# Forget-gate logits with the gate weights stationary in four column tiles of the array, summed and turned back by two products with a picking matrix

## The chip, the cores and the metric

One core of one Trainium2 chip. The time is the device time of one execution in microseconds; lower is better. TensorE (PE) multiplies, VectorE (DVE), ScalarE (ACT) and GpSimd (POOL) do the rest, SyncE (SP) issues most of the DMA transfers.

## What is computed

The reference is a model of two layers on 256 tokens of width 1024, all in float32. Each layer is a modulated norm, an attention block, a second norm and a mixture of 32 experts, of which each token uses two. The change touches one small piece of layer 0: eight of its sixteen attention heads have forget gates. Their logits are the last eight columns of the input projection, and their running sum over the tokens goes into the scores.

```python
proj = h @ w_in                       # h: 256 x 1024; w_in: 1024 x 3080, the last 8 columns are fb
log_f = jax.nn.log_sigmoid((fb + b_f).astype(jnp.float32))
cum_f = jnp.transpose(jnp.cumsum(log_f, axis=1), (0, 2, 1))
...
s = (jnp.einsum('bqhd,bkhd->bhqk', qb[:, i0:i1], kb[:, :i1]).astype(jnp.float32) * scale
     + (cum_f[:, :, i0:i1, None] - cum_f[:, :, None, :i1]))
```

## The kernel before

The program is written engine by engine, with semaphores between them; nothing reorders it. The activations of a layer lie turned in `m.hT`: 128 partitions by 8 chunks of the model width by 256 tokens. Dense weights come in units of 2 MB through a ring of six slots, in the order of `DENSE_ORDER`; SyncE issues a unit's transfer when the slot is free (`ring_used`).

In layer 0, once `m.hT` is ready, TensorE runs `project_early`: six items, each one unit's 512 columns for one half of the tokens (8 products of 128x512, line 642). Unit in0 gives items 0 and 1, in1 items 2 and 3, in2 items 4 and 5. Between them stand:

- after item 0, `forget_gates` (line 650): for each half of the tokens 8 products with a 128x128 piece of `m.hT` stationary and the 128x8 gate weights moving, so that the 128x8 logits lie with tokens on partitions;
- after items 1 and 3, `mod_products` of the group GATE1 (line 607): 8 products with 32 columns of the conditioning vector stationary, in four column tiles of 32 columns, moving 512 columns of weights;
- from item 2 on, `turn_qk` (line 697): transposes of queries and keys that VectorE has normed;
- after item 4, `forget_sums` (lines 658 to 664): the running sums, as products with a triangular matrix. Then attention starts (`scores`, line 734), with the other six items spread over its steps.

A product in float32 shows as two instructions in the trace. ScalarE copies each item out (`copy_item`), does the exponential and the logarithm of the gates (`f_abs`, `f_exp`) right after item 0, and the square root of each norm (`root8`). VectorE waits for the logits (`forget`, line 1407), then norms items 0 to 3 (`norm_qk`, lines 1426 to 1451). It has one order too: `forget` stands ahead of `norm_qk(0)`.

The small inputs, the gate weights among them, are loaded by ScalarE's queue at the start (`small_loads`, line 543); `forget_gates` waits for all nine of them on TensorE, and VectorE waits for them before it makes the rotary angles. After attention comes the router (line 844), and then the experts of the layer, whose weights stream through eight slots of 2 MB.

Of the kernel before, what the change touches and what calls it, by code (L numbers as in the profile page):

```python
# [26 lines left out]
P = 128  # L27
# [132 lines left out]
class Chain:  # L160
# [5 lines left out]
    def link(self, ins):  # L166

        self.n += 1
        ins.then_inc(self.sem, 1)
        self.eng.wait_ge(self.sem, self.n + self.more)  # L170
# [6 lines left out]
def allocate(nc, ctx):  # L177
    m = Machine()

    def sb(name, shape, dt=F32):  # L180
        return ctx.enter_context(nc.sbuf_tensor(name, shape, dt))

    def sem(name):
# [36 lines left out]
    m.cos, m.sin = (m.region[:, 6 * D + COL + 64 * i:6 * D + COL + 64 * (i + 1)].rearrange("p (t e) -> p t e", t=TT)  # L220
                    for i in range(2))
    m.head_g = m.region[:, 6 * D + COL + 128:6 * D + COL + 384].rearrange("p (i e) -> p i e", i=4)
    m.f_w = m.region[:, 6 * D + COL + 384:6 * D + COL + 448].rearrange("p (k h) -> p k h", k=KC)

    m.raw = [m.work[:, i * COL:(i + 1) * COL] for i in range(2)]
# [33 lines left out]
    m.cum_q = sb("cum_q", [P, TT, 8])  # L260
    m.cum_k = m.h[:, 1, 0:T]
    m.log_f2 = m.h[:, 1, T:2 * T].rearrange("p (t h) -> p t h", t=TT)
    m.sq_sum = sb("sq_sum", [P, 8])
    m.rstd = sb("rstd", [P, 8])
    m.low = sb("low", [P, NHH, TT])
# [26 lines left out]
    m.dve_step = sem("dve_step")  # L292
    m.act_step = sem("act_step")
    m.pool_step = sem("pool_step")
    names = """consts eps_ready gate_b_clear rows_ready c_act_done c_ready part_ready cols_made cols_ready row_made row_ready
        rstd_done h0_ready h1_ready hT_turned hT_dve hT_act
        proj_done proj_copied var8_ready rstd8_done qk_normed qk_turned qk_copied f_out f_abs f_exp f_ln f_ready cum_done cum_copied
        ang_ready trig_done lam_ready lam_exp
# [162 lines left out]
def program_pool(pool, m):  # L461
# [5 lines left out]

    pool.memset(m.eps[:, :], EPS).then_inc(m.s["eps_ready"], 1)
    pool.memset(m.ones[:, :], 1.0).then_inc(done, 1)
    pool.memset(m.gate_b[:, :], 0.0).then_inc(m.s["gate_b_clear"], 1)  # L470
    pool.memset(m.hot[:, :], 0.0).then_inc(step, 1)
    pool.memset(m.pick[:, :, :], 0.0).then_inc(step, 1)
# [18 lines left out]
    for b in range(4):  # L491
        ins = mask(m.pick[:, b % 2, :], [[0, P]], 1, ALU.not_equal, 1.0, base=-32 * b)
        ins.then_inc(step if b < 2 else done, 1)
        if b == 1:
            pool.wait_ge(step, 11)

    pool.wait_ge(m.s["hT_turned"], TT)
    pool.memset(m.head_row, 0.0).then_inc(step, 1)
    pool.memset(m.log_f2, 0.0).then_inc(m.s["rows_ready"], 1)
    pool.wait_ge(step, 12)  # L500
    for b in range(2):
        mask(m.head_row, [[-1, 8], [0, P]], 1, ALU.not_equal, 1.0, base=-64 * b).then_inc(
            step if b == 0 else m.s["rows_ready"], 1)
        pool.wait_ge(step, 13)

    pool.wait_ge(m.s["sc_moved"], NHH)
    pool.memset(m.carry[:, :], 1.0).then_inc(step, 1)
    pool.wait_ge(step, 14)
    for lo, base in ((0, -1), (P, P - 1), (2 * P, -1)):
        mask(m.carry[:, lo:lo + P], [[-1, P]], 1, ALU.is_gt, 0.0, base=base).then_inc(m.s["carry_ready"], 1)  # L510

# [20 lines left out]
def small_loads(act, m, a):  # L532

    got = m.got["small"]
    act.dma_start(m.pos_i[:, :], a["positions"].rearrange("b (t p) -> p (b t)", p=P),
                  allow_slow_non_contiguous=True).then_inc(got, 16)
    for i, n in enumerate(("ev_qn_a", "ev_kn_a", "ev_qn_b", "ev_kn_b")):
        act.dma_start(m.head_g[:, i, :], spread(a[n][0])).then_inc(got, 16)
    act.dma_start(m.sub_g[:, :], a["ev_subln_g"][0].rearrange("(p a) -> p a", a=1)).then_inc(got, 16)
    act.dma_start(m.lam_in[:, :, :], spread(a["ev_lam"][0])).then_inc(got, 16)  # L540
    act.dma_start(m.f_b[:, :], spread(a["ev_b_f"][0])).then_inc(got, 16)
    w_in = a["ev_w_in"][0].rearrange("(p k) n -> p k n", k=KC)
    act.dma_start(m.f_w[:, :, :], w_in[:, :, IN_UNITS * COL:IN_UNITS * COL + 8]).then_inc(got, 16)

def router_loads(eng, m, a):
# [38 lines left out]
def program_tensor(pe, m):  # L585
# [58 lines left out]
        return last  # L644

    def forget_gates():
        pe.wait_ge(m.got["small"], 16 * SMALL_LOADS)
        for t in range(TT):
            for k in range(KC):
                last = pe.matmul(bank[7][:, 8 * t:8 * t + 8], m.hT[:, k, t * P:(t + 1) * P], m.f_w[:, k, :],  # L650
                                 start=(k == 0), stop=(k == KC - 1))
        last.then_inc(s["f_out"], 1)

    def forget_sums():
# [46 lines left out]
    def project_early(l):  # L701

        for i in range(EARLY_ITEMS):
            project_item(l, i)
            if l == 0 and i == 0:
                forget_gates()
            if i >= 2 and l == 0:
                turn_qk(i - 2)
            if l == 0 and i == 4:
                forget_sums()  # L710
            if i in (1, 3):
                mod_products(l, GATE1, i // 2)
# [363 lines left out]
def program_scalar(act, m, a):  # L1076
# [75 lines left out]
    def project_early(l):  # L1152
        for i in range(EARLY_ITEMS):
            copy_item(l, i)
            if l == 0 and i == 0:
                act.wait_ge(s["f_abs"], 1)
                chain.link(fn(m.f_t[:, 1], m.f_t[:, 1], ACT.Exp, scale=-1.0))
                fn(m.f_t[:, 1], m.f_t[:, 1], ACT.Ln, bias=1.0).then_inc(s["f_ln"], 1)
            if i >= 2 and l == 0:
                copy_qk(i - 2)  # L1160
            if l == 0 and i < 4:
                root8(i)
# [164 lines left out]
def program_vector(dve, m):  # L1327
# [72 lines left out]

    def heads(ap, n):
        return ap.rearrange("p (h e) -> p h e", h=n)

    def forget():
        dve.wait_ge(s["f_out"], 1)
# [309 lines left out]
    for l in range(DEPTH):  # L1715
# [4 lines left out]
        if l == 0:  # L1720
# [2 lines left out]
            lambdas()  # L1723
            keep = 1.0 - (0.8 - 0.6 * math.exp(-0.3 * 0))
            link(ts(m.sub_g[:, :], m.sub_g[:, :], keep, None, ALU.mult))
            forget()
            for i in range(4):
                norm_qk(i)
            forget_sums()
            mod_part(0, GATE1)  # L1730
# [62 lines left out]
```

## Time and profile before

| | us |
|---|---|
| median of 3 runs | 1326.66 (1325.58 to 1328.46) |
| the profiled execution's own time | 1328.47 |
| its span on the engines | 1326.7 |
| TensorE busy | 934.0 (70% of the span) |
| VectorE busy | 262.4 (20%) |
| ScalarE busy | 203.6 (15%) |
| GpSimd busy | 30.2 (2%) |

### The profile page before, as it was taken

To read this page: it belongs to the slowest core of one execution; us is meant where nothing else is said; L and a number is where in the kernel's file an instruction comes from. 1 tells how busy PE (TensorE), PEld (TensorE's weight loads), DVE (VectorE), ACT (ScalarE), POOL (GpSimd) and SP (SyncE) were. 2 spreads that over 40 slices of the span, in tenths; PEclk is the share of its full clock that TensorE was granted. 3 is DMA by queue.
4 is the path that set the end of the run, shared out by engine and by line. 5 is a ranking of instruction groups with operands and counts; after the bars stand their busy time and mean duration, and the time that the engine had idled before them with its cause. 6 is when DMAs were issued, how large, how long until landed. Compare 5 with 4: busy or idle time off the path is not lost.

```text
span 1326.7 us, 13670 instructions
## 1 busy us (share of the span) xinstructions
PE 934.0 (70%) x5664; PEld 429.9 (32%) x5664; DVE 262.4 (20%) x573; ACT 203.6 (15%) x423; POOL 30.2 (2%) x89
## 2 busy tenths in 40 slices
PE   4999899556565746556679998995563755655486
PEld 1444455122221212122237665442120212213131
DVE  0445545011010101011020367421010101101011
ACT  2212424010110001000110344230100101010000
POOL 3000000000000000000000022000000000000000
PEclk9799999787887878788989999987886868877888
DMA  9984648999999999999999447489999999999995
GB/s 356 381 263 181 233 162 331 389 429 427 428 428 429 428 428 428 428 426 429 421 408 380 160 164 317 175 369 429 428 427 428 429 429 429 428 428 427 429 423 239
DMA packets 67575, 489.98 MB, mean 369 GB/s; under 512 B 18240, under 2 KB 18368, under 8 KB 37576
## 3 DMA queue, kind: packets, MB, share of 16 engines
q1 hardware_dynamic: 64512, 487.95, 88.9%
q10 hardware_dynamic: 3016, 1.37, 0.4%
q8 instruction: 34, 0.56, 0.2%
q14 instruction: 13, 0.11, 0.0%
HBM read 488.25 MB, written 1.05 MB: 369 GB/s over the span
## 4 chain that ended last, share of the span: by engine, by line
DMA 49%; PE 43%; DVE 3%; SPq 2%; issue 1%; ACT 1%; DVEq 0%
DMA tokens<-in_moe_w_dram 44%; PE bank L881 12%; PE bank L642 9%; PE bank L910 5%; PE bank L682 4%; PE bank L794 4%; DMA ring<-in_mod_w_dram 4%; PE bank L607 2%; SPq L400 2%; DMA ring<-in_moe_w_dram 2%; PE bank L734 1%; PE bank L636 1%; PE bank L844 1%; PE bank L850 1%; ACT att L1081 1%
## 5 line engine op out<-in xcount | busy, mean ns | idle before, releaser
L881 PE MATMUL bank<-ring,region 128*32 128x512 f32 x1472 | 258.9, 664 | 168.5 <-DMA tokens<-in_moe_w_dram 85.4
L910 PE MATMUL bank<-ring,region 128*32 128x512 f32 x832 | 148.4, 741 | 150.5 <-DMA ring<-in_moe_w_dram 97.8
L881 PEld LDWEIGHTS bank<-ring,region 128*32 128x32 f32 x1472 | 69.1, 121 | 343.5 <-issue 276.9
L881 PE MATMUL bank<-work,region 128*32 128x512 f32 x256 | 131.5, 673 | 0.0
L881 PE MATMUL bank<-tokens,region 128*32 128x512 f32 x256 | 131.5, 673 | 0.0
L642 PE MATMUL bank<-ring,tokens 128*128 128x512 f32 x256 | 119.8, 621 | 2.7 <-ACT tokens L1081 2.7
L910 PEld LDWEIGHTS bank<-ring,region 128*32 128x32 f32 x832 | 38.8, 132 | 247.6 <-issue 211.9
L1672 DVE TENSOR_TENSOR region<-region,bank 128x512 f32<-128x512 f32 x16 | 11.0, 688 | 434.6 <-PE bank L881 434.6
L1081 ACT ACTIVATE region<-bank,shift,scale 128x128 f32<-128x128 f32 x64 | 24.0, 456 | 381.3 <-PE bank L868 381.3
L1679 DVE TENSOR_TENSOR region<-bank,region 128x512 f32<-128x512 f32 x32 | 20.6, 686 | 289.5 <-PE bank L910 289.5
L642 PEld LDWEIGHTS bank<-ring,tokens 128*128 128x128 f32 x256 | 49.4, 199 | 62.3 <-issue 59.6
L868 PE MATMUL bank<-region,h 128*128 128x128 f32 x512 | 63.4, 285 | 8.6 <-issue 7.8
L919 PE MATMUL bank<-region 128*128 128x512 f32 x128 | 59.2, 605 | 14.1 <-DVE region L1679 14.1
L868 PEld LDWEIGHTS bank<-region,h 128*128 128x128 f32 x512 | 62.6, 201 | 16.2 <-issue 15.2
L607 PE MATMUL bank<-ring,c_wide 128*32 128x512 f32 x368 | 49.2, 660 | 18.7 <-DMA ring<-in_mod_w_dram 18.7
L682 PE MATMUL bank<-tokens,ring 128*128 128x256 f32 x256 | 59.9, 394 | 2.7 <-ACT tokens L1081 2.7
L794 PE MATMUL bank<-ring,tokens 128*128 128x512 f32 x128 | 57.3, 597 | 0.4 <-issue 0.3
L910 PE MATMUL bank<-work,region 128*32 128x512 f32 x96 | 55.9, 748 | 0.0
L910 PE MATMUL bank<-tokens,region 128*32 128x512 f32 x96 | 55.9, 748 | 0.0
L682 PEld LDWEIGHTS bank<-tokens,ring 128*128 128x128 f32 x256 | 50.0, 198 | 11.8 <-ACT tokens L1081 2.7
L1260 ACT COPY region<-bank 128x256 f32<-128x256 f32 x16 | 6.0, 372 | 291.2 <-PE bank L893 291.2
L919 PEld LDWEIGHTS bank<-region 128*128 128x128 f32 x128 | 23.0, 189 | 51.9 <-DVE region L1679 29.0
(230 smaller groups left out, 867.3 us busy)
## 6 DMA issues: line engine op xcount, KB each, us to landing
ring<-in_moe_w_dram SPq DMA_DIRECT2D x144, 2048.0 KB, 19.5
ring<-in_mod_w_dram SPq DMA_DIRECT2D x23, 2048.0 KB, 12.6
work<-in_moe_w_dram SPq DMA_DIRECT2D x22, 2048.0 KB, 24.2
tokens<-in_moe_w_dram SPq DMA_DIRECT2D x22, 2048.0 KB, 28.6
ring<-in_ev_w_in_dram SPq DMA_DIRECT2D x6, 2048.0 KB, 22.4
ring<-in_od_w_in_dram SPq DMA_DIRECT2D x6, 2048.0 KB, 19.9
alone<-in_moe_w_dram SPq DMA_DIRECT2D x2, 2048.0 KB, 11.9
ring<-in_ev_w_out_dram SPq DMA_DIRECT2D x2, 2048.0 KB, 7.9
```

The source lines that it names most:

```text
L400: sp.dma_start(unit_tile(m.slots[slot], u, halves), expert_unit(m, a, l, quad, u, halves)).then_inc(m.ring_full[slot], 16)
L607: last = pe.matmul(out[32 * j:32 * j + 32, :], m.c_wide[:, k, :], w[:, k - rows * e, i * COL:(i + 1) * COL], start=first, stop=end, skip_g ...
L636: last = pe.transpose(turned_at(bank, n, k, t), m.h[:, t, k:D:KC], m.ident[:, :])
L642: last = pe.matmul(bank[b][:, 0:cols], m.hT[:, k, t * P:(t + 1) * P], w[:, k, :], start=(k == 0), stop=(k == KC - 1))
L682: last = pe.matmul(bank[proj_bank(i)][:, c * T:(c + 1) * T], w[:, k, lo:lo + P], m.hT[:, k, :], start=(k == 0), stop=(k == KC - 1))
L794: last = pe.matmul(bank[out_bank(half, i)][:, :], m.hT[:, 4 * half + k, t * P:(t + 1) * P], w[:, k, u * COL:(u + 1) * COL], start=(k == 0) ...
L868: last = pe.matmul(bank[2 + k // 4][:, (k % 4) * P:(k % 4 + 1) * P], m.h[:, t, k * P:(k + 1) * P], m.sel[:, t, :], start=(t == 0), stop=(t ...
L881: last = pe.matmul(bank[which][32 * j:32 * j + 32, :], m.seated[:, k, 32 * j:32 * j + 32], weights(4 * which + j, k * FE), start=(k == 0), ...
L910: last = pe.matmul(bank[half][32 * j:32 * j + 32, :], m.hidT[:, c, 32 * j:32 * j + 32], w, start=(c == 0), stop=(c == FC - 1), skip_group_ ...
L919: last = pe.matmul(bank[4 + 2 * half + t][:, :], m.back[:, t, :], m.y_seat[:, half * COL:(half + 1) * COL], start=False, stop=end is not N ...
L1081: return act.activation(out, in_, f, **kw)
L1679: tt(m.y_seat[:, cols], bank[half][:, :], m.gate2[:, cols], ALU.mult).then_inc(e["y_copied"], 1)
```

## The change

The gate weights become the stationary operand. Each chunk k of the model width has a tile of 32 columns in `m.f_wide`, the 8 gates and 24 zeros; eight products move the 256 tokens of `m.hT` through it, chunk k in column tile k mod 4. Bank 7 then holds four partial sums, at partitions 0, 32, 64 and 96, with tokens along the free axis. VectorE copies them to `m.f_part` (128x256). After item 1, two products with 128 tokens of `m.f_part` stationary and the picking matrix `m.f_pick` moving (128x8; a one where the partition is the gate, or the gate plus 32, 64 or 96) add the four and turn them, so that the 128x8 logits lie where they lay. VectorE norms item 0 before it waits for them, and ScalarE does `root8(0)` and `copy_item(1)` before their exponential. GpSimd clears `m.f_wide` at the start and makes `m.f_pick` after the other constants; the load of the gate weights waits for the clearing and now lands in pieces of 8 of 32 columns.

```diff
     m.head_g = m.region[:, 6 * D + COL + 128:6 * D + COL + 384].rearrange("p (i e) -> p i e", i=4)
-    m.f_w = m.region[:, 6 * D + COL + 384:6 * D + COL + 448].rearrange("p (k h) -> p k h", k=KC)
+    m.f_wide = m.region[:, 7 * D - 64:7 * D + 192].rearrange("p (k h) -> p k h", k=KC)
+    m.f_pick = m.region[:, 7 * D + 192:7 * D + 200]
...
+    m.f_part = m.h[:, 1, 2 * T:3 * T]
...
+    pool.memset(m.f_wide[:, :, :], 0.0).then_inc(m.s["f_clear"], 1)
...
+    pool.memset(m.f_pick, 0.0).then_inc(step, 1)
+    for b in range(4):
+        pool.wait_ge(step, 12 + b)
+        mask(m.f_pick, [[-1, 8]], 1, ALU.not_equal, 1.0, base=-32 * b).then_inc(step if b < 3 else m.s["f_pick_ready"], 1)
...
+    act.wait_ge(m.s["f_clear"], 1)
+    act.dma_start(m.f_wide[:, :, 0:8], w_in[:, :, IN_UNITS * COL:IN_UNITS * COL + 8]).then_inc(got, 16)
...
     def forget_gates():
+
+
         pe.wait_ge(m.got["small"], 16 * SMALL_LOADS)
+        for k in range(KC):
+            j = k % 4
+            last = pe.matmul(bank[7][32 * j:32 * j + 32, P:P + T], m.f_wide[:, k, :], m.hT[:, k, :],
+                             start=(k < 4), stop=(k >= 4), skip_group_check=True, tile_position=(0, 32 * j))
+        last.then_inc(s["f_turned"], 1)
+
+    def forget_turns():
+
+        pe.wait_ge(s["f_copied"], 1)
+        pe.wait_ge(s["f_pick_ready"], 1)
         for t in range(TT):
-            for k in range(KC):
-                last = pe.matmul(bank[7][:, 8 * t:8 * t + 8], m.hT[:, k, t * P:(t + 1) * P], m.f_w[:, k, :],
-                                 start=(k == 0), stop=(k == KC - 1))
+            last = pe.matmul(bank[7][:, 8 * t:8 * t + 8], m.f_part[:, t * P:(t + 1) * P], m.f_pick, start=True, stop=True)
         last.then_inc(s["f_out"], 1)
 
     def forget_sums():
@@ -704,6 +722,8 @@
             project_item(l, i)
             if l == 0 and i == 0:
                 forget_gates()
+            if l == 0 and i == 1:
+                forget_turns()
             if i >= 2 and l == 0:
...
-            if l == 0 and i == 0:
+            if l == 0 and i == 1:
...
 
+    def copy_forget():
+        dve.wait_ge(s["f_turned"], 1)
+        dve.tensor_copy(m.f_part, bank[7][:, P:P + T]).then_inc(s["f_copied"], 1)
...
             link(ts(m.sub_g[:, :], m.sub_g[:, :], keep, None, ALU.mult))
+            copy_forget()
+            norm_qk(0)
             forget()
-            for i in range(4):
+            for i in range(1, 4):
```

On TensorE, in `project_early` of layer 0, before (line 650 is `forget_gates`, 642 an item, 607 `mod_products`, 697 `turn_qk`):

```order
L642 MATMUL bank<-ring,tokens 128x512 x8
L650 MATMUL bank<-region,tokens 128x8 x16
L642 MATMUL bank<-ring,tokens 128x512 x8
L607 MATMUL bank<-ring,c_wide 32x512 x8
L642 MATMUL bank<-ring,tokens 128x512 x8
L697 MATMUL bank<-ident,work 128x128 x4
```

and with the change (660 is `forget_gates`, 669 `forget_turns`, 650 an item, 615 `mod_products`, 715 `turn_qk`):

```order
L650 MATMUL bank<-ring,tokens 128x512 x8
L660 MATMUL bank<-tokens,region 32x256 x8
L650 MATMUL bank<-ring,tokens 128x512 x8
L669 MATMUL bank<-region,h 128x8 x2
L615 MATMUL bank<-ring,c_wide 32x512 x8
L650 MATMUL bank<-ring,tokens 128x512 x8
L715 MATMUL bank<-ident,work 128x128 x4
```

Sixteen products with 8 moving columns became eight with 256 in column tiles of 32, and two with 8 moving columns stand behind item 1.

On VectorE, from the end of the setup on, before (1407 to 1414 are `forget`, 1426 to 1451 `norm_qk`):

```order
L1725 TENSOR_SCALAR sub_g<-sub_g 128x1
L1407 TENSOR_TENSOR f_t<-bank,f_b 128x16
L1408 TENSOR_SCALAR f_t<-f_t 128x16
L1409 TENSOR_TENSOR f_t<-f_t 128x16
L1411 SCALAR_TENSOR_TENSOR log_f<-f_t 128x16
L1414 COPY h<-log_f 128x2x8 x2
L1426 TENSOR_TENSOR work<-work 128x512
L1427 TENSOR_REDUCE sq_sum<-work 128x8
L1429 TENSOR_TENSOR work<-work,rstd 128x512
L1437 TENSOR_TENSOR work<-work,region 128x512
L1445 TENSOR_TENSOR work<-work,region 128x8x32
L1446 TENSOR_TENSOR work<-work,region 128x8x32
```

and with the change (1426 is `copy_forget`, 1431 to 1438 `forget`, 1450 to 1475 `norm_qk`):

```order
L1426 COPY h<-bank 128x256
L1450 TENSOR_TENSOR work<-work 128x512
L1451 TENSOR_REDUCE sq_sum<-work 128x8
L1453 TENSOR_TENSOR work<-work,rstd 128x512
L1461 TENSOR_TENSOR work<-work,region 128x512
L1469 TENSOR_TENSOR work<-work,region 128x8x32
L1470 TENSOR_TENSOR work<-work,region 128x8x32
L1471 TENSOR_TENSOR work<-work,region 128x8x32
L1473 TENSOR_TENSOR work<-work,region 128x8x32
L1474 TENSOR_TENSOR work<-work 128x8x32
L1475 TENSOR_TENSOR work<-work 128x8x32
L1431 TENSOR_TENSOR f_t<-bank,f_b 128x16
```

The whole of `norm_qk(0)` moved ahead of `forget`, and a copy of 128x256 out of a bank stands ahead of both.

## Rows read from the trace of the kernel before

**Rows 1.** The page, part 4: the chain that ended last, by engine.
```profile
DMA 49%; PE 43%; DVE 3%; SPq 2%; issue 1%; ACT 1%; DVEq 0%
```

**Rows 2.** The chain of waits, 22 to 100 us: start us, us, what.
```profile
23.06 2.73 PE bank L607 x16
...
45.12 3.95 PE bank L650 x32
49.07 9.86 PE bank L642 x16
58.93 1.85 PE bank L607 x16
60.78 7.06 PE bank L642 x16
67.85 0.44 PE bank L697 x4
68.28 6.87 PE bank L642 x16
...
85.07 0.22 PE bank L659 x2
...
94.41 0.93 PE bank L734 x8
```

**Rows 3.** Windows of 20 us in the attention of layer 0.
```profile
120.00:140.00 20.00, 19.97 (x79) 10.53 (x78) 12.33 (x32) 8.70 (x29) 0.00 (x0) 1.00 0.37 135
```

**Rows 4.** The chain of waits, 0 to 300 us.
```profile
230.26 14.06 PE bank L881 x128
...
245.54 34.74 DMA tokens<-in_moe_w_dram
```

**Rows 5.** Windows of 2 us: busy time per engine, PEclk, DMA share, GB/s.
```profile
44.00:46.00 2.00, 2.00 (x14) 1.43 (x12) 0.00 (x0) 0.58 (x1) 0.00 (x0) 1.00 1.06 418
46.00:48.00 2.00, 2.00 (x20) 2.00 (x20) 0.00 (x0) 0.00 (x0) 0.00 (x0) 0.98 1.00 401
48.00:50.00 2.00, 2.00 (x8) 1.48 (x8) 0.53 (x3) 0.20 (x1) 0.00 (x0) 0.50 1.04 402
...
54.00:56.00 2.00, 2.00 (x5) 0.91 (x4) 1.93 (x6) 0.00 (x0) 0.00 (x0) 0.81 1.05 387
```

**Rows 6.** Timeline of TensorE: start us, us, line, operands, count.
```profile
216.03 1.98 PE L844 MATMUL bank<-r_w,tokens 128*128 128x36 f32 x16
```

**Rows 7.** Windows of 2 us behind the router's products.
```profile
218.00:220.00 2.00, 2.00 (x6) 1.01 (x6) 1.38 (x9) 1.11 (x1) 0.00 (x0) 0.65 1.05 451
```

**Rows 8.** Timeline of VectorE; in brackets the idle time before and its releaser.
```profile
49.17 0.17 DVE L1407 TENSOR_TENSOR f_t<-bank,f_b 128x16 f32<-128x16 f32 x1 [7.48 <-PE bank L650]
...
50.30 0.18 DVE L1411 SCALAR_TENSOR_TENSOR log_f<-f_t 128x16 f32<-128x16 f32 x1 [0.53 <-ACT f_t L1081]
...
56.06 0.42 DVE L1451 TENSOR_TENSOR work<-work 128x256 f32<-128x256 f32 x1
59.65 0.69 DVE L1426 TENSOR_TENSOR work<-work 128x512 f32<-128x512 f32 x1 [3.17 <-ACT work L1135]
...
86.49 0.41 DVE L1419 TENSOR_SCALAR h<-bank 128x256 f32<-128x256 f32 x1
```

**Rows 9.** Windows of 1 us around the first modulation products.
```profile
24.00:25.00 1.00, 1.00 (x12) 0.07 (x4) 0.00 (x0) 0.00 (x0) 0.00 (x0) 0.52 0.98 402
...
27.00:28.00 1.00, 1.00 (x9) 1.00 (x8) 0.00 (x0) 0.00 (x0) 0.00 (x0) 0.77 1.04 379
```

**Rows 10.** Timeline of ScalarE's DMA issues (ACTq).
```profile
7.74 0.63 ACTq L543 DMA_DIRECT2D region<-in_ev_w_in_dram  x1
```

**Rows 11.** Transfers around 7.8 us: size, us from issue to landing.
```profile
region<-in_ev_w_in_dram ACTq DMA_DIRECT2D x1, 32.0 KB, 29.1
```

**Rows 12.** Timeline of SyncE's DMA issues (SPq).
```profile
23.53 4.09 SPq L386 DMA_DIRECT2D ring<-in_ev_w_in_dram  x1
```

**Rows 13.** Transfers around 23 us: size, us from issue to landing.
```profile
ring<-in_ev_w_in_dram SPq DMA_DIRECT2D x1, 2048.0 KB, 22.9
```

More of the change, by code:

```diff
@@ L294, in allocate @@
     m.pool_step = sem("pool_step")
-    names = """consts eps_ready gate_b_clear rows_ready c_act_done c_ready part_ready cols_made cols_ready row_made row_ready
+    names = """consts eps_ready gate_b_clear f_clear f_pick_ready f_turned f_copied rows_ready c_act_done c_ready part_ready cols_made cols_ready row_made row_ready
         rstd_done h0_ready h1_ready hT_turned hT_dve hT_act
@@ L499, in program_pool @@
     pool.memset(m.log_f2, 0.0).then_inc(m.s["rows_ready"], 1)
-    pool.wait_ge(step, 12)
+    pool.wait_ge(step, 16)
     for b in range(2):
@@ L503, in program_pool @@
             step if b == 0 else m.s["rows_ready"], 1)
-        pool.wait_ge(step, 13)
+        pool.wait_ge(step, 17)
     pool.wait_ge(m.s["sc_moved"], NHH)
     pool.memset(m.carry[:, :], 1.0).then_inc(step, 1)
-    pool.wait_ge(step, 14)
+    pool.wait_ge(step, 18)
     for lo, base in ((0, -1), (P, P - 1), (2 * P, -1)):
@@ L542, in small_loads @@
     w_in = a["ev_w_in"][0].rearrange("(p k) n -> p k n", k=KC)
-    act.dma_start(m.f_w[:, :, :], w_in[:, :, IN_UNITS * COL:IN_UNITS * COL + 8]).then_inc(got, 16)
+    act.wait_ge(m.s["f_clear"], 1)
+    act.dma_start(m.f_wide[:, :, 0:8], w_in[:, :, IN_UNITS * COL:IN_UNITS * COL + 8]).then_inc(got, 16)
 def router_loads(eng, m, a):
```

## The prediction

> **What bounds the kernel now.** I read first the page's chain that ended last: 49% of the span is DMA and 43% is TensorE [rows 1]. An average of that kind hides stages with different limits, so I then followed the chain in order of time. From 45 to 93 us every piece of it is TensorE, one group of products behind the other with no gap [rows 2]. The weights are not what it waits for there: in the attention that follows, the 16 DMA engines are busy for 0.37 of the time, while TensorE is busy for 19.97 of 20 us [rows 3]. The ring is full and the transfers wait for TensorE to free slots. DMA comes onto the chain again only behind the first products of the experts, at 245.54 [rows 4], with a transfer that those products release. So what TensorE saves at 45 us should reach the end whole: attention, router, experts and the second layer all start from it.
>
> The place of the change is the 3.95 us that `forget_gates` (line 650) takes between items 0 and 1 [rows 2]. I then asked for windows of the granted clock around it. It was 1.00 in 44:46 and 0.98 in 46:48, 0.50 in 48:50 and 0.81 in 54:56 [rows 5]. At two levels only, 0.98 means that it fell 0.08 us before 48, at 47.92; 0.81 means that it stayed low for 0.76 us after 54, to 54.76. It fell though TensorE counted as busy for every instant of 44 to 50. What was special is the kind of work: 8 moving columns behind each 128-column weight load. Item 1 pays for it: 9.86 us, where the two items at full clock take 7.06 (behind a column-tiled group) and 6.87 [rows 2]. The same happens once more behind narrow products: the router's, with 36 columns (16 instructions in 1.98 us, [rows 6]), are followed by a clock of 0.65 in 218:220 [rows 7].
>
> **The change, part by part.**
>
> *Removed:* 32 instructions, 3.95 us on the chain [rows 2].
>
> *Added, eight column-tiled products of 256 columns.* The nearest row is `mod_products` (line 607): eight products of 512 columns in four column tiles, 16 instructions in 1.85 us between two items, both switches of the tiling included [rows 2]. An item's 16 instructions of 512 columns take 6.87 us, 0.429 each; a quarter of that is 0.107, and 16 times 0.107 is 1.72, so 0.13 of the 1.85 is fixed. With half of the columns I get 0.86 + 0.13 = 0.99 us. Bounds: 0.93 (all of it halves) and 1.85 (none does). I take 0.99, since this row differs in nothing but the width.
> The Trainium skill (TensorEngine Tiling (Array Packing), section Key Properties) says that changing the tiling mode drains TensorE, which speaks against putting such a group between two items of full width. The 0.13 us above is what this trace shows for it; the page gives no duration, so by it the sum would be the same or a little worse.
>
> *Added, two products with 8 moving columns.* The same form is line 659: one product, two instructions, 0.22 us [rows 2]. Two are 0.44; from the removed group, 3.95/16, they would be 0.49. They wait for VectorE's copy. The tiled group ends at 46.1; a copy of 128x256 out of a bank takes 0.41 [rows 8], so it is done by 46.6, while the turns come at 53. That wait is covered by item 1; uncovered it would cost 0.5 us. 3.95 - 0.99 - 0.44 = **2.52 us** less work.
>
> *The clock.* In place of 3 us of narrow products TensorE now has 1 us of column-tiled ones and goes on with item 1. Do column-tiled products keep the clock up? At 23.06 they start behind idle time and are followed at 25.8 by transposes; the clock is 0.52 in 24:25 and comes up in 27:28 (0.77) [rows 2, 9], so a stretch that holds such products was enough to raise it. And after the group at 58.93 the next item takes 7.06 [rows 2]. So I expect full clock through item 1: 6.95, the middle of 6.87 and 7.06, instead of 9.86, **2.91 us** less. Check: 5.69 us of item 1 lay in the low stretch (49.07 to 54.76); half of it is 2.85.
>
> *Moved, on VectorE.* Before, `forget` began at 49.17 and had its last step but one at 50.30, behind 0.53 us of waiting for ScalarE's exponential and logarithm; `norm_qk(0)` ended at 56.48, and VectorE then stood idle for 3.17 us before `norm_qk(1)` at 59.65 [rows 8]. So `forget` is some 1.5 to 1.7 us, and the norm some 5.8. Now `norm_qk(0)` starts near 46.6 and is done by 52.5. The logits come at 53.5; `forget` takes as long as before, so `norm_qk(1)` starts at 55.2. Its raw input is there at about 53.7. Behind VectorE's wait for the logits stands only that norm, and who wants it is the transpose after item 3, at about 69.8; with 6 us for the norm there are 8 us to spare. ScalarE waits inside the same 1.7 us, ahead of `root8(1)`, which is on the same path. Nothing of this is late.
>
> *Moved and added elsewhere.* GpSimd's clearing of 256 columns and of the picking matrix, and four masks of 8 columns, lie before 23.06, where TensorE waits for weights; the price is zero under that cover. The load of the gate weights was issued at 7.74 and took 29.1 us to land, at 36.8 [rows 10, 11]; TensorE wants it at 45.1. Its pieces in memory stay 8 floats long, so I expect no other landing. Of the units, in1 was issued at 23.53 and landed 22.9 later, at 46.4 [rows 12, 13]. It is wanted now at 55.4 instead of 60.78: 9 us to spare; GATE1's first unit, issued ahead of it on the same queue, is wanted at 53.5.
>
> **The sum.** Item 0 ends at 45.12. 45.12 + 0.99 + 6.95 + 0.44 = 53.50, where GATE1 now starts, instead of 58.93: 5.43 us less. From the profiled execution's own time, 1328.47, that gives 1323.04. The runs' median, 1326.66, lies 1.81 below it; the same step from there gives 1321.23. Where in a run the clock falls need not be the same in each execution, and the profiled one may have had more of the low stretch than most. I take the middle, 1322.1.
>
> **The rivals.**
>
> *The clock is not regained.* Then only the work is saved, 2.52: 1325.95 from the profiled time, 1324.14 from the median. For it: the cause of the drop is read off two places, and column-tiled products use a quarter of the array's columns each. Against it: the rise at 27 and the item behind 58.93 [rows 2, 9]. The Trainium skill (TensorE: Matmul & The Clock Gate, section Why this matters for your kernels) asks for no idle gaps between bursts of products; taken alone, by that rule the old stretch, with no gap in it, would have cost no clock, and the change could give none back. The trace disagrees with that as a full account: 2.00 of 2.00 us busy, and the clock fell. I give this case 0.15.
>
> *The column tiles do not overlap* at this width. Then each costs half of an item's product, 0.43, eight 3.47, with the turns 3.91: no work saved, only the clock: 2.95 less, 1325.5 (1323.7 from the median). Line 607's 1.85 us for what would be 6.87 untiled speaks against it. 0.05.
>
> *Slower:* the gate weights land late. They now go into pieces of 8 of 32 columns; if this made the 32 KB slower to write, TensorE would stand still after item 0, and VectorE too, which waits for all nine small loads before its angles. The landing at 36.8 may slip by 8.3 us for nothing, and by 8.3 + 5.4 = 13.7 us before the change loses; beyond 50.5 us each microsecond is lost whole. A landing twice as long, 58 us from the issue, would end at 65.9 and cost 15.4 net: 1343.9. The number and the length of the pieces read do not change. 0.03.
>
> **How the numbers follow.** The forecast has 0.77, the rivals 0.15, 0.05 and 0.03. The low end of the range is the sum from the median with 1 us for what another run's clock does elsewhere, 1320.2. The high end, 1325.4, takes in most of the cases in which only one of the two terms comes true. About 0.2% (2.65 us) is what a measurement of this kernel tells from no change. The forecast clears it by 2.8 us, but if most runs before had only half of the low stretch, it clears it by little; the work alone (2.52) is just below it, the clock alone (2.95) just above. Faster by over 0.2%: 0.80; within: 0.16; slower: 0.04.
>
> **What would show it.** In the profile after: the tiled group takes 0.9 to 1.1 us; the clock reads 1.00 from 44 through 58; item 1 takes 6.9 to 7.1; the two turns take 0.4 to 0.5 with no idle time before them; GATE1 starts near 53.5; attention's first scores start near 89.0 instead of 94.41 [rows 2]. The forecast is wrong if a 0.50 stands in the windows of item 1, if the turns wait for the copy, if item 0 is followed by a wait for a transfer, or if the 5.4 us are there at 60 us and gone behind the router.

## The result

| | before | changed |
|---|---|---|
| median of 4 runs | 1326.12 us (1325.10 to 1328.46) | 1318.13 us (1316.26 to 1318.40) |
| the profiled execution's own time | 1328.47 | 1316.26 |
| its span | 1326.7 | 1314.5 |
| TensorE busy | 934.0 | 921.3 |
| VectorE busy | 262.4 | 263.4 |
| GpSimd busy | 30.2 | 31.4 |

The ratio is 0.9944, with a 95% interval of 0.9917 to 0.9970: 8.0 us less, where 4.0 (1322.1) was forecast, and below the low end of the range. Later series of both kernels, on other chips too, put this in proportion. Over 109 runs the kernel before has a mean of 1323.5 us, and its runs fall into two groups: 50 under 1323.5 with a mean of 1320.8, and 59 above with a mean of 1325.9 (the lower and the upper group from here on; no run lies between 1322.3 and 1323.7). Over 24 runs the changed kernel has a mean of 1318.7, and its highest run is at 1321.8. The difference of the means is 4.9 us (4.1 to 5.6); within the two later series that have both kernels on one chip it is 4.4 and 5.5. The four runs before in the table all belong to the upper group, and so do the three of them on which the forecast was built.

### The profile page after: what moved, and what is told of

It is laid out like the page before. It is cut to its first block, busy times and chain, and to the rows that moved or that the text cites. A ratio compares the mean times of both kernels' runs of the same rounds, so it can differ in the third digit from the quotient of the medians.

```text
span 1314.5 us, 13658 instructions
## 1 busy us (share of the span) xinstructions
PE 921.3 (70%) x5652; PEld 422.4 (32%) x5652; DVE 263.4 (20%) x574; ACT 203.7 (15%) x423; POOL 31.4 (2%) x95
## 4 chain that ended last, share of the span: by engine, by line
DMA 50%; PE 41%; DVE 4%; SPq 2%; issue 2%; ACT 1%; DVEq 0%
DMA tokens<-in_moe_w_dram 40%; PE bank L901 10%; PE bank L650 9%; DMA ring<-in_moe_w_dram 6%; PE bank L930 6%; PE bank L700 4%; PE bank L814 4%; DMA ring<-in_mod_w_dram 4%; SPq L402 2%; PE bank L615 2%; PE bank L754 1%; ACT att L1101 1%; PE bank L864 1%; PE bank L770 1%; PE bank L939 1%
## 5 line engine op out<-in xcount | busy, mean ns | idle before, releaser
L650 PE MATMUL bank<-ring,tokens 128*128 128x512 f32 x256 | 115.3, 602 | 2.7 <-ACT tokens L1101 2.7
L814 PE MATMUL bank<-ring,tokens 128*128 128x512 f32 x128 | 57.3, 598 | 0.4 <-issue 0.3
```

What stands on the lines that cost most here:

```text
L650: last = pe.matmul(bank[b][:, 0:cols], m.hT[:, k, t * P:(t + 1) * P], w[:, k, :], start=(k == 0), stop=(k == KC - 1))
L814: last = pe.matmul(bank[out_bank(half, i)][:, :], m.hT[:, 4 * half + k, t * P:(t + 1) * P], w[:, k, u * COL:(u + 1) * COL], start=(k == 0) ...
```

## The profile after

The page's part 4, the chain that ended last by engine, is like that of [rows 1]:

```profile
DMA 50%; PE 41%; DVE 4%; SPq 2%; issue 2%; ACT 1%; DVEq 0%
```

The chain of waits in the stretch of the change (line 650 is an item now, 660 the column-tiled group, 669 the two turns, 615 the modulation products, 754 the scores):

```profile
34.97 8.54 PE bank L650 x16
43.51 1.00 PE bank L660 x16
44.51 7.06 PE bank L650 x16
51.58 0.34 PE bank L669 x4
51.92 1.85 PE bank L615 x16
...
87.40 0.93 PE bank L754 x8
```

Against [rows 2]: the gates take 1.00 instead of 3.95 us, item 1 7.06 instead of 9.86, the turns 0.34. From the end of item 0 to the start of GATE1's products 13.81 us became 8.41, so 5.40 us are gone; the sum said 5.43. Ahead of that place nothing should differ, but item 0 itself takes 8.54 us from 34.97 to 43.51, where it took 10.17 before (34.95 to 45.12).

The windows of 2 us, columns as in [rows 5], show full clock where 0.50 stood:

```profile
44.00:46.00 2.00, 2.00 (x16) 0.87 (x9) 1.31 (x3) 0.14 (x1) 0.00 (x0) 1.00 1.04 411
46.00:48.00 2.00, 2.00 (x6) 0.80 (x6) 1.36 (x3) 0.51 (x2) 0.00 (x0) 1.00 1.01 402
...
50.00:52.00 2.00, 2.00 (x12) 1.13 (x14) 0.77 (x2) 0.39 (x1) 0.00 (x0) 1.00 1.06 390
```

VectorE, timeline; in brackets the idle time and what ended it (1355 are the rotary angles, 1426 the copy, 1431 the gates, 1450 the norm of an item):

```profile
38.18 0.17 DVE L1355 CAST pos<-pos_i 128x2 f32<-128x2 int32 x1 [3.31 <-DMA region<-in_ev_w_in_dram]
...
44.65 0.42 DVE L1426 COPY h<-bank 128x256 f32<-128x256 f32 x1 [1.66 <-PE bank L660]
...
52.03 0.17 DVE L1431 TENSOR_TENSOR f_t<-bank,f_b 128x16 f32<-128x16 f32 x1 [1.23 <-PE bank L669]
...
61.57 0.69 DVE L1450 TENSOR_TENSOR work<-work 128x512 f32<-128x512 f32 x1 [2.22 <-ACT work L1155]
```

The copy takes 0.42 us and is over by 45.1, 6.5 us ahead of the turns. VectorE waits 1.23 us for the logits and is idle for 2.22 us before the norm of item 2, so the new order is covered. The first of these rows is the rival in which the small loads land late: VectorE waited for them until 38.18, 1.3 us later than before; TensorE, which needs them at 43.5, had 5 us left. The delay is no sure effect of the new pieces: `order_alone` and `split_narrow`, which load the weights as before, have 37.7 and 37.8.

The rest of the 12.2 us between the two profiled executions lies where nothing was changed. The table gives the stages as the timelines of TensorE have them: from the first product of item 0 to the first scores (with the change in it), on to the router of layer 0, to the first expert products, to the router of layer 1, to its first expert products, and to the end of the span.

| profiled execution (own time) | item 0 to scores | to router 0 | to experts 0 | to router 1 | to experts 1 | to the end |
|---|---|---|---|---|---|---|
| before (1328.47) | 59.46 | 119.41 | 16.44 | 630.80 | 17.97 | 447.67 |
| changed (1316.26) | 52.43 | 119.05 | 15.38 | 630.26 | 16.58 | 445.83 |
| before, b_again (1325.92) | 59.12 | 119.58 | 16.39 | 630.20 | 17.97 | 445.86 |
| before, b_third (1321.00) | 54.51 | 120.46 | 15.21 | 630.40 | 16.43 | 446.10 |
| before, b_fourth (1319.84) | 54.73 | 120.44 | 15.19 | 630.62 | 16.42 | 446.08 |
| changed, a_again (1319.12) | 53.92 | 120.46 | 15.38 | 630.30 | 16.58 | 445.99 |
| changed, a_third (1321.05) | 52.70 | 118.19 | 18.18 | 630.57 | 18.13 | 446.07 |

Between the first two rows 7.0 us came in the first stage, and another 5.2 in the later ones. The lower rows are the repeats, told below.

## The experiments

**The changed kernel again, and the kernel before again.** Where do the other 2.6 us of the 8.0 come from? No edit. What was expected of `a_again`:

> The changed kernel once more, with a new profile. The change gave 8.0 us in the medians and 12.2 between the two profiled executions, where its own place accounts for 5.4 us (2.95 at the gates, 2.8 in item 1, the turns 0.34). Two theories for the rest. Luck: stretches at half clock elsewhere differ from execution to execution, item 0 (10.17 us before, 8.54 after) and both router stages among them; then this profile may show item 0 anywhere from 8.5 to 10.2, the mean over many runs tends to 5 to 6 us faster than before, ratio 0.995 to 0.996. System: the changed kernel always has item 0 near 8.5, and the ratio stays at 0.9935 to 0.994.

and of `b_again`:

> The kernel before once more, with a new profile, as a control. Luck: ratio 1.000 within 0.001, and item 0 or the router's stages take another time than in the first profile (item 0 10.17 us). System: item 0 takes 10.1 to 10.2 us again, with the clock coming up near 41 us. Under both theories the 3.95 us of narrow products are followed by a stretch at half clock in item 1, of 3 to 7 us.

`a_again` gave a median of 1318.98 against 1324.19 for 35 runs before: ratio 0.9972 (0.9957 to 0.9986). (The ratio is not the quotient of the two medians, which is 0.9961 here: where the runs fall into two groups, the two differ by 0.001 or so.) Its mean is 4.4 us below that of the 35 runs. `b_again` gave 1323.37, ratio 1.0003 (0.9985 to 1.0022). Timeline of TensorE, `a_again` (items, line 650; tiled group, 660):

```profile
34.77 10.02 PE L650 MATMUL bank<-ring,tokens 128*128 128x512 f32 x16 [2.65 <-ACT tokens L1101]
44.73 1.07 PE L660 MATMUL bank<-tokens,region 128*32 128x256 f32 x16
45.73 7.13 PE L650 MATMUL bank<-ring,tokens 128*128 128x512 f32 x16
```

Item 0 takes 10.02 us in it, as it did before, and 8.54 in the first profile of the same code. So its length is no effect of the change: of the two theories, luck. Item 1 is at 7.06 again, though the clock came up as late as in `b_again` (0.84 in 40:42, where `b_again` has 0.85). Timeline and windows of `b_again` (items, line 642; gates, 650):

```profile
35.08 9.84 PE L642 MATMUL bank<-ring,tokens 128*128 128x512 f32 x16 [2.65 <-ACT tokens L1081]
44.76 4.41 PE L650 MATMUL bank<-region,tokens 128*128 128x8 f32 x32
49.02 9.70 PE L642 MATMUL bank<-ring,tokens 128*128 128x512 f32 x16
```

```profile
46.00:48.00 2.00, 2.00 (x18) 2.00 (x17) 0.00 (x0) 0.00 (x0) 0.00 (x0) 0.85 1.04 414
48.00:50.00 2.00, 2.00 (x7) 1.49 (x7) 0.52 (x3) 0.10 (x1) 0.00 (x0) 0.50 1.02 394
```

The half-clock stretch is there again, behind the narrow products: item 1 takes 9.6 us. These two profiles make the plainest comparison of the series: item 0 alike, the clock at full in 42:46 in both, and only the one with narrow products behind it loses the clock.

**The kernel before, a third and a fourth time,** for their profiles.

> The kernel before a third time, for its profile alone. Two profiles so far, both of runs in the upper group (1328.47, 1325.92), show item 1 at 9.86 and 9.63 us. If this execution is of the lower group (under 1323), item 1 should be near 7 us, or the half-clock stretch in it much shorter; if the two groups come from another place, item 1 is 9.6 or more in the lower group too.

> The kernel before once more for its profile. Three profiles: 1328.47 and 1325.92 with item 1 at 9.9 and 9.6 us and the second router at 17.97 us to the experts' first products, 1321.00 with item 1 at 7.0 and that stage at 16.4. If this execution is above 1324, both should be long again; below 1322, both short.

They came at 1321.00 and 1319.84, both in the lower group. Timeline and windows of `b_third`:

```profile
36.19 8.60 PE L642 MATMUL bank<-ring,tokens 128*128 128x512 f32 x16 [2.65 <-ACT tokens L1081]
44.62 3.63 PE L650 MATMUL bank<-region,tokens 128*128 128x8 f32 x32
48.11 7.11 PE L642 MATMUL bank<-ring,tokens 128*128 128x512 f32 x16
```

```profile
46.00:48.00 2.00, 2.00 (x21) 2.00 (x20) 0.00 (x0) 0.00 (x0) 0.00 (x0) 1.00 1.03 413
48.00:50.00 2.00, 2.00 (x8) 1.04 (x8) 1.00 (x7) 0.43 (x2) 0.00 (x0) 1.00 1.01 395
```

The same 16 narrow products, no wait between, and the clock reads 1.00 in all windows from 40 to 56: the gates take 3.5 us and item 1 7.0. `b_fourth` has item 1 at 6.97 and the gates at 3.47 in its chain. This shows where most of the 5 us between the groups lies: item 0 to the scores is 59.1 to 59.5 us in the upper executions, 54.5 to 54.7 in the lower. About 3.4 us of it are the gates and item 1 (13.81 and 13.80 us against 10.44); item 0 itself, ahead of the narrow products, has another 1.0 to 1.6 (9.84 and 10.17 us against 8.60 and 8.81). The stage behind router 1 goes with it as expected, 17.97 and 16.4.

**The clock alone.** The narrow products stay but are divided; VectorE and ScalarE have the new order.

```diff
-    def forget_gates():
+    def forget_gates(t):
...
-            if l == 0 and i == 0:
-                forget_gates()
+            if l == 0 and i < 2:
+                forget_gates(i)
```

> The kernel before with its 16 narrow products kept but divided: eight behind item 0 (2 us), eight behind item 1 (2 us), VectorE and ScalarE in the order of the changed kernel. The same work on TensorE, so this is the clock term alone. If a long unbroken run of narrow products is what lowers the clock: item 1 takes 6.9 to 7.1 us and the time is 2.8 us below before (ratio 0.998), more if the rest of the gain is systematic. If the clock falls for another reason (a place in time): item 1 takes 9.9 us again and the ratio is 1.000.

Timeline of TensorE (narrow products, line 649; item 1, 642):

```profile
43.59 1.85 PE L649 MATMUL bank<-region,tokens 128*128 128x8 f32 x16
45.30 7.11 PE L642 MATMUL bank<-ring,tokens 128*128 128x512 f32 x16
52.25 1.85 PE L649 MATMUL bank<-region,tokens 128*128 128x8 f32 x16
```

Median 1321.03, ratio 0.9986 (0.9972 to 1.0000), no run above 1323.2. In the profile two narrow runs of 1.7 us did not lower the clock, and item 1 takes 6.97 in the chain. By itself that decides nothing: item 0 takes 8.63 us in this execution, and where it was that short, in `b_third` and `b_fourth`, the undivided run did not lower the clock either. The run times carry the finding. None of twelve lies in the upper group; at 59 of 109 that would come up by chance less than once in a thousand series. The mean, 1321.2, is 2.4 us (1.6 to 3.1) below the mean before. The work on TensorE is the same, so this is the clock term in the mean; at this place it is about 3.4 us in an execution of the upper group (13.81 us for gates and item 1 against 10.44) and nothing in one of the lower.

**The work alone, made wide.** All eight products of 256 columns in one column tile; only 32 partitions are copied and turned.

```diff
-            j = k % 4
-            last = pe.matmul(bank[7][32 * j:32 * j + 32, P:P + T], m.f_wide[:, k, :], m.hT[:, k, :],
-                             start=(k < 4), stop=(k >= 4), skip_group_check=True, tile_position=(0, 32 * j))
+            last = pe.matmul(bank[7][0:32, P:P + T], m.f_wide[:, k, :], m.hT[:, k, :],
+                             start=(k == 0), stop=(k == KC - 1), skip_group_check=True, tile_position=(0, 0))
```

> The changed kernel with all eight products of 256 columns in one column tile of 32, so that nothing overlaps: 3.44 us (half of an item) instead of 1.00. Work like before, but wide. Clock theory: the clock stays at 1.00 through item 1, the time is 2.4 us above the changed kernel (ratio to before 0.9955 to 0.9965). If narrow stationary operands (32 of 128 columns) also lower the clock: item 1 takes 9 us or more and the time is 5 us above the changed kernel (ratio 0.998).

```profile
43.83 3.64 PE L659 MATMUL bank<-tokens,region 128*32 128x256 f32 x16
47.40 7.13 PE L650 MATMUL bank<-ring,tokens 128*128 128x512 f32 x16
```

The group takes 3.57 us in the chain instead of 1.00, so the column tiles do overlap, 3.6 times. Item 1 stays at 7.06 in this profile, but item 0 takes 8.80 us in it, as in the lower executions of the kernel before: whether a stationary operand of 32 columns would keep the clock up in an execution of the other kind is not shown. Median 1322.10, ratio 0.9998 (0.9981 to 1.0015), where 0.9955 to 0.9965 was expected: a miss. The mean of 1322.5 is 3.9 (2.5 to 5.4) above the changed kernel; the chain gives 2.57 + 0.2, which lies inside. Two of the twelve runs, 1325.6 and 1327.9, are longer than the slowest run of the changed kernel with 2.8 added, so a fall of the clock somewhere in some executions is not ruled out; the one profile is of the fastest, 1319.48.

**A narrow stretch put back, and a wide one of the same length.** Behind the tiled group of the changed kernel, into columns that nobody reads:

```diff
+        for k in range(12):
+            pe.matmul(bank[6][:, 0:8], m.hT[:, k % KC, 0:P], m.f_wide[:, k % KC, 0:8], start=True, stop=True)
```

> The changed kernel with twelve further products of 8 moving columns behind the column-tiled group (into columns that nobody reads), 2.96 us by the 0.247 of one in the kernel before: a narrow stretch of the old length, everything else new. Clock theory: the runs fall into two groups as those of the kernel before do (19 of 35 at 1324 to 1327, 16 at 1319.5 to 1322.3), the lower near 1321, the upper near 1326; a profile of the upper one shows item 1 at 9.7 to 9.9 us. If the narrow products have nothing to do with the two groups: one group, 3.0 us above the changed kernel, 1321 to 1323.

and in the other kernel instead:

```diff
+        for k in range(7):
+            pe.matmul(bank[6][:, 0:T], m.hT[:, k % KC, 0:P], m.hT[:, k, :], start=True, stop=True)
```

> The changed kernel with seven further products of 256 moving columns at that place, 3.0 us (0.43 each): the same time of added work as the narrow products, but wide. Clock theory: one group of runs near 1321.5, item 1 at 6.9 to 7.1 us, PEclk 1.00 from 44 to 58, no run above 1324 that repeats. If any added 3 us before item 1 brings the upper group back: two groups, 5 us apart.

`add_narrow`: mean 1324.0, 8 of 12 runs above 1323.5, ratio 1.0006 (0.9992 to 1.0020). `add_wide`: mean 1321.9, 3 of 12 above, ratio 0.9988 (0.9974 to 1.0002). (With 3 us added, runs of the changed kernel would reach 1325, so the count says less here than the mean; two runs, 1324.4 and 1326.3, lie above the 1324 named.) The wide products cost 3.25 us (2.1 to 4.5) over the changed kernel, as they should; the narrow ones, shorter in work by 0.45 us in the chain, cost 2.1 (0.5 to 3.7) more than that. The profile of `add_narrow`, an execution of 1325.66, does not show what was expected of it:

```profile
45.59 2.85 PE L664 MATMUL bank<-region,tokens 128*128 128x8 f32 x24
48.29 7.11 PE L650 MATMUL bank<-ring,tokens 128*128 128x512 f32 x16
```

Item 1 takes 6.97 in the chain there, at full clock. What made that execution long is elsewhere (121.5 us to router 0, 630.6 from experts 0 to router 1, 18.13 behind router 1, where `add_wide` has 120.5, 628.7 and 16.6). So the upper times do not come from item 1 alone: a time near 1326 can also be made up of other stretches. And that the 2.1 us come from a fall behind the added products is not shown; no profile has it. `add_wide`:

```profile
44.94 3.29 PE L664 MATMUL bank<-tokens 128*128 128x256 f32 x14
48.07 7.03 PE L650 MATMUL bank<-ring,tokens 128*128 128x512 f32 x16
```

**The order on VectorE and ScalarE alone**, TensorE as before:

```diff
+            norm_qk(0)
             forget()
-            for i in range(4):
+            for i in range(1, 4):
...
-            if l == 0 and i == 0:
+            if l == 0 and i == 1:
                 act.wait_ge(s["f_abs"], 1)
```

> The kernel before with the new order on VectorE and ScalarE only (norm of item 0 ahead of the gates), TensorE as before. It lay beside TensorE's work in my sum: ratio 1.000, the same two groups of runs as before, 5 us apart. If this order is what gives part of the gain, the median falls by 1 us or more and both groups move.

Median 1323.42, ratio 0.9995 (0.9981 to 1.0008), six of 12 runs above 1323.5: both groups where they were. Its profile shows the fall of the clock as before:

```profile
44.72 4.43 PE L650 MATMUL bank<-region,tokens 128*128 128x8 f32 x32
49.00 9.68 PE L642 MATMUL bank<-ring,tokens 128*128 128x512 f32 x16
```

**The changed kernel a third time, and the same form for the router.** The profiles left a second place with a long narrow run, the router's 16 products of 36 columns in each layer. Its kernel is the changed one with:

```diff
-                pe.matmul(b, m.hT[:, k, t * P:(t + 1) * P], m.r_w[:, l, k, :], start=(k == 0), stop=False)
+                pe.matmul(bank[1][64 * j:64 * j + LOGITS, t * P:(t + 1) * P], m.r_w[:, l, k, :],
+                          m.hT[:, k, t * P:(t + 1) * P], start=(k < 2), stop=(k == KC - 1),
+                          skip_group_check=True, tile_position=(0, 64 * j))
...
+        mod_row(l, GATE2, 1)
+        pe.wait_ge(s["r_copied"], l + 1)
...
+            last = pe.matmul(b, m.att[0:64 + LOGITS, 2 * D + t * P:2 * D + (t + 1) * P],
+                             m.r_pick[0:64 + LOGITS, :], start=True, stop=True)
```

> The changed kernel a third time, for the mean over more runs and a third profile. Over 80 runs the kernel before has a mean of 1323.58, the changed one over 16 runs 1318.74: 4.8 us. Luck theory: this series stays at a mean of 1318 to 1320, none of its runs in the group at 1325 to 1327, ratio 0.996 to 0.997, and item 0 takes anything from 8.4 to 10.2 us. If the 8.0 us of the first series were what the change is worth, the ratio would be at 0.994.

> The changed kernel with the same form for the router of both layers: 36 logit columns stationary in two column tiles of 64, the partial sums copied by VectorE beside the 512-wide row product, two products with a picking matrix. By the rows of the changed kernel the logits take 1.95 + 0.34 + 1.91 + 0.35 = 4.55 us from 206.45 to 211.0 now; tiled, two groups of 0.9 us, the row product 0.86 over the copy of 0.42, two turns 0.5: ready at about 210.3, 0.7 us earlier in each layer, 1.4 us in all. Clock theory: no narrow run is left before the products that place x (4.66 us at a clock partly low, 3.5 at full), which adds up to 1 us per layer in the executions that have it: mean 1.4 to 3 us below the changed kernel, 1316 to 1317.5. Rival: the wait for the second half of the tokens and the copy's latency eat the gain: 1318.5 to 1319.5, and the window behind the router shows full clock without the time moving.

`a_third`: median 1317.87, ratio 0.9956 (0.9937 to 0.9975), mean 1318.5, nothing above 1321.1. Its profile has a fall of the clock that the change does not touch. Timeline and a window at router 0 (864 are the router's products, 636 the row product, 870 those that place x):

```profile
206.35 1.95 PE L864 MATMUL bank<-r_w,tokens 128*128 128x36 f32 x16
...
208.56 2.62 PE L864 MATMUL bank<-r_w,tokens 128*128 128x36 f32 x16
...
211.69 2.08 PE L636 MATMUL bank<-region,pick 128*128 128x512 f32 x2
213.55 5.08 PE L870 MATMUL bank<-tokens,ident 128*128 128x512 f32 x8
```

```profile
210.00:212.00 2.00, 2.00 (x9) 1.86 (x9) 0.17 (x2) 1.63 (x1) 0.00 (x0) 0.50 1.05 442
```

The clock fell inside the second eight narrow products (2.55 us in the chain instead of 1.91) and stayed at half through the row product and most of x. That stage took 18.18 us, 2.8 more than in the other two profiles of the changed kernel. The tiled router (869 the products, 880 the turns, 885 x):

```profile
208.45 1.07 PE L869 MATMUL bank<-tokens,r_w 128*36 128x128 f32 x16
...
209.79 1.07 PE L869 MATMUL bank<-tokens,r_w 128*36 128x128 f32 x16
...
212.09 0.53 PE L880 MATMUL bank<-r_pick,att 100*128 100x36 f32 x4
212.45 3.68 PE L885 MATMUL bank<-tokens,ident 128*128 128x512 f32 x8
```

```profile
210.00:212.00 2.00, 2.00 (x20) 1.22 (x17) 0.42 (x1) 2.00 (x2) 0.00 (x0) 1.00 1.01 434
```

Full clock, and 14.86 us to the experts. The full clock alone is no proof: two of the three profiles of the changed kernel have it there too, with 15.38 us. `router_tiled` had a mean of 1318.3 over 8 runs, ratio 0.9956 (0.9939 to 0.9973), where 1316 to 1317.5 was expected. Eight runs do not tell it from the changed kernel, so it ran again:

> The router-tiled kernel once more, for its mean and a second profile. Eight runs gave a mean of 1318.3, against 1318.7 over 24 runs of the changed kernel: not told apart. If the 0.5 us of path and the clock stretches of both routers count, the mean over both series comes out at 1316.5 to 1317.7; if they are given back (another place where the clock falls, or the experts' transfers), it stays at 1318.0 to 1318.7. In the profile both routers should read PEclk 1.00 until the products that place x are done, and take 14.8 to 15.0 us up to the experts' first products.

`router_again`: median 1316.85, ratio 0.9951 (0.9930 to 0.9972). Both routers take 14.86 and 14.83 us in both profiles, where the three profiles of the changed kernel have 15.4 to 18.2. The mean over 15 runs is 1317.9, 0.8 us below the changed kernel (0.1 above to 1.7 below): not clear of noise, and between the two ranges expected. Part is given back in layer 1: from the experts' first products to the end the two take 447.4 and 447.7 us, where the changed kernel has 445.8 to 446.1. The chain of waits shows a transfer taking over there. In layer 1 of `router_tiled` (885 is x, 916 the experts) it runs:

```profile
858.32 3.53 PE bank L885 x8
...
861.91 14.68 DMA tokens<-in_moe_w_dram
876.59 0.04 issue
876.64 7.20 PE bank L916 x64
```

Behind x the chain is a transfer of expert weights, issued once x is placed, and TensorE stands idle for 0.58 us until it has landed, at 876.64; in `a_again` no transfer stands on the chain between the router and the experts' first 128 products, which end at 885.48. So part of what the router saves is given back at that transfer. Whether it accounts for all of the 1.5 us or so was not tried.

**All profiles at the place of the change.** The repeats say together what no single one does. Before the narrow products, in item 0, the clock comes up at a time that differs between executions. It can be worked out from the windows as in the prediction, at two levels; two of the rows, of the kernel before and of `b_third`:

```profile
40.00:42.00 2.00, 2.00 (x5) 0.79 (x4) 0.31 (x2) 1.30 (x2) 0.00 (x0) 0.72 1.05 390
```

```profile
38.00:40.00 2.00, 2.00 (x5) 0.96 (x4) 1.73 (x9) 0.53 (x3) 0.00 (x0) 0.70 1.05 396
```

| profile | item 0, us | clock up at | behind item 0 | starts at | clock falls at | item 1, us |
|---|---|---|---|---|---|---|
| before | 10.17 | 41.1 | 16 narrow | 45.12 | 47.9 | 9.86 |
| b_again | 9.84 | 40.6 | 16 narrow | 44.92 | 47.4 | 9.55 |
| order_alone | 9.82 | 40.5 | 16 narrow | 44.88 | 47.4 | 9.53 |
| b_third | 8.60 | 39.2 | 16 narrow | 44.78 | no | 6.97 |
| b_fourth | 8.81 | 38.1 | 16 narrow | 43.43 | no | 6.97 |
| router_again | 10.16 | 41.1 | tiled | 45.12 | no | 7.06 |
| a_again | 10.02 | 40.6 | tiled | 44.80 | no | 7.06 |
| add_narrow | 9.66 | 40.1 | tiled, 12 narrow | 44.66 | no | 6.97 |

In the three executions in which the clock came up at 40.5 to 41.1 us and the 16 narrow products followed, it fell. In the two in which it came up at 38.1 and 39.2, it did not. With the tiled group behind item 0 it stayed up although it had come up at 40.6 and 41.1. `add_narrow` lies between: up at 40.1, a narrow run of 2.77 us from 45.66 on, no fall; whether the run's length or its place spared it is not shown. `router_again`, whose code up to this place is that of the changed kernel, is the twin of the first profile of the kernel before: item 0 ends at 45.12 in both, and then

```profile
45.12 1.00 PE bank L665 x16
46.12 7.06 PE bank L655 x16
```

stand against 3.95 and 9.86 in [rows 2]. These pairs show that the form of the gates' products decides about the clock, in the executions in which it comes up late. The other profiles (the first of the changed kernel, `a_third`, `router_tiled`, `split_narrow`, `one_tile`, `add_wide`) have the clock up by 39.2 or, for `router_tiled`, 40.0 with a later item 0; in such executions item 1 is at 6.9 to 7.1 whatever stands before it. What makes it come up late in one execution and early in another was not tried.

## Why the prediction was wrong, point by point

**The sum at the place of the change was right.** It said 2.52 us less work and 2.91 for the clock. Measured between the two profiles: 3.95 - 1.00 - 0.34 = 2.61, and 9.86 - 7.06 = 2.80 (less 0.01 of issue). The tiled group was forecast at 0.99 and took 1.00; the bounds 0.93 and 1.85 were needless. The turns, forecast at 0.44 from line 659, took 0.34. GATE1 was to start at 53.50 and did at 51.92, 1.58 earlier; item 0 alone made 1.61 of that. (Eight times 0.43 is 3.44, not the 3.47 of the second rival; nothing hangs on it, and the untiled group measured 3.57.)

**Its split into work and clock was not.** The 3.95 us of the gates were counted as work whole, though the clock had fallen at 47.92, inside them. At full clock they take 3.47 (`b_third`, `b_fourth`). So the work saved is 3.47 - 1.00 - 0.34 = 2.13 us, and with item 1 at 7.06 instead of 6.97 an execution of the lower group gains 2.04 us at this place; one of the upper group gains 5.40.

**The covers held.** No wait for the copy, none for a transfer, the new order beside TensorE's work (`order_alone`: no difference).

**The cause of the fall was right.** Where the clock comes up late, the 16 narrow products in one run are followed by its fall (three profiles of three), and the tiled group in their place is not (`a_again`, `router_again`). That two short runs do not lower it either rests on the run times of `split_narrow`; for wide products (`one_tile`, `add_wide`) no profile of such an execution exists. The rival in which the clock is not regained is out: all five profiles with the tiled group, those of the tiled router among them, have item 1 at 7.06. The rule that asks for no idle gaps (the Trainium skill, TensorE: Matmul & The Clock Gate, section Why this matters for your kernels) does not describe this: TensorE was busy for 2.00 of 2.00 us as the clock fell. But it does not fall every time, and that the prediction did not see: `b_third` and `b_fourth` have the narrow run and no fall. In the mean the clock term is 2.4 us (1.6 to 3.1), not 2.91.

**What failed is the step from the sum to a time.** "The profiled one may have had more of the low stretch than most. I take the middle, 1322.1", and the low end was "the sum from the median with 1 us for what another run's clock does elsewhere". Both took the clock's luck elsewhere for small, on the strength of three runs within 2.9 us: the term was sized at 1 us. But in one and the same code item 0 takes 8.5 to 10.0 us, the stage behind router 0 15.4 to 18.2, the one behind router 1 16.6 to 18.1, and the kernel before as a whole has two groups of runs 5.0 us apart. The three runs all came from the upper group. From the group's mean of 1325.9 the sum gives 1320.4, and the changed kernel's mean is 1318.7, lower by another 1.7. The profiles point to where that lies: item 0 takes 9.8 to 10.2 us in the upper profiles of the kernel before and 8.5, 8.8 and 10.0 in the changed kernel, and the stage behind router 1 takes 17.97 in the upper ones and 16.58 in two of three of the changed. The first profile of the changed kernel, 1316.26, is a further 2.4 below its mean. The mean over many runs, 4.9 us less, is near the 5.4 of the sum, but part of that is luck: the sum holds for the upper group only. With 2.04 us in 50 of 109 runs and 5.40 in 59 the place of the change gives 3.9 us, and the other 1.0 us (0.2 to 1.8) has no cause that was shown.

Of those 8.0 us, then, about 5 are the change. The other 3 are most likely the draw: with 59 of 109 runs in the upper group, four out of four come up about one time in twelve (0.54 to the fourth power is 0.086), if the runs are independent.

## What to carry to other kernels

Look at the granted clock behind every group of products with few moving columns, also where TensorE has no idle time. Swap the operands so that the long side moves and pack them into column tiles, or at least break the run with wide products: the last costs no work, and none of its twelve runs here was in the upper group.

Before a forecast leans on a median, ask whether the runs are one group. If the clock can fall in some executions and not in others, take several profiles, compare means over dozens of runs, and set side by side only profiles that agree up to the place of the change: a profile in which the kernel before would have kept its clock too proves nothing about the clock.

## What the runs showed of the hardware

- The same 3.5 us of 8-column products are followed by a half-clock stretch in some executions (0.50 in 48:50, item 1 9.5 to 9.9 us, three of five profiles with this order on TensorE) and by none in others (1.00, 7.0 us). In the three the clock had come up at 40.5 to 41.1 us, in the two at 38.1 and 39.2. In the two profiles in which it came up at 40.6 and 41.1 and a column-tiled group followed, it stayed at 1.00. Two runs of 1.7 us had no fall in the one profile taken, in which the clock had come up at 38.2.
- One kernel on one core can have two groups of run times, here 1320.8 and 1325.9 in the mean, over the same instructions.
- Eight products of 256 columns take 1.00 us in four column tiles and 3.57 in one.
- A product that turns the four partial sums (128x8 moving) took 0.17 us, less than the 0.22 of line 659 in [rows 2]; over 32 partitions, in `one_tile`, it took 0.27.
